# The first norm's scale and shift made as columns on TensorE, rows normalised and turned early

## The reference, cut to what matters

```python
cond = jax.nn.silu(c)                                   # 1 x 1024
mod = cond @ ada_w[layer] + ada_b[layer]                # ada_w: 1024 x 6144 for each layer
sh1, sc1, g1, sh2, sc2, g2 = jnp.split(mod, 6, axis=-1)
h = rms_norm(x, norm_mix[layer]) * (1 + sc1) + sh1      # the "first norm" of a layer
mix = mix_gla_gdn(h, ab_w_in[i], ...)                   # layer 0: begins with h @ ab_w_in
...
```

## Time and profile before

| what | value |
|---|---|
| median of 3 runs | 1464.72 us (1463.73 to 1470.1) |
| profiled execution, span | 1464.9 us |
| TensorE busy, share of the span | 87% |
| VectorE busy | 75% |
| ScalarE busy | 47% |
| first instruction of the first projection on TensorE | 62.41 us from the start |

### The profile page before, as it was taken

One profiled execution on the slowest core, in us unless ns is written; L12 is line 12 of the kernel. 1 busy time (PEld: TensorE's weight loads), 2 busy tenths in 40 slices (PEclk: granted clock), 3 DMA queues, 4 the chain that ended last, 5 costly groups with the idle time before them and its releaser, 6 DMA issues. The chain is left out here.

```text
span 1464.9 us, 15502 instructions
## 1 busy us (share of the span) xinstructions
PE 1280.1 (87%) x6000; PEld 970.2 (66%) x6000; DVE 1101.5 (75%) x1324; ACT 693.7 (47%) x890; POOL 311.9 (21%) x129
## 2 busy tenths in 40 slices
PE   4798997859899959999999967986898799999992
PEld 1476885659884557888888754444446588888882
DVE  2757986667783657999999946967357499999994
ACT  2222344222251316777777714227522377777770
POOL 2100000000000001555555310000000145555541
PEclk9799998979999959999999977997996799999997
DMA  9788626011703257999999546354006499999955
GB/s 328 259 266 272 214 96 211 19 44 58 259 2 130 87 219 273 375 391 382 373 378 373 225 157 240 115 203 183 1 29 258 142 358 385 377 381 392 380 206 191
DMA packets 63856, 338.17 MB, mean 231 GB/s; under 512 B 11837, under 2 KB 12350, under 8 KB 49700
## 3 DMA queue, kind: packets, MB, share of 16 engines
q1 hardware_dynamic: 51428, 311.00, 57.3%
q0 software_dynamic: 11536, 22.91, 4.5%
q10 hardware_dynamic: 816, 3.23, 0.6%
HBM read 325.64 MB, written 28.84 MB: 242 GB/s over the span
## 5 line engine op out<-in xcount | busy, mean ns | idle before, releaser
L1421 PE MATMUL ps<-ring_r,work_r 128*128 128x512 f32 x536 | 212.7, 397 | 0.0
L2455 DVE TENSOR_TENSOR ring_r<-ring,early_mod_r 128x2048 fp32r<-128x2048 f32 x76 | 188.7, 2512 | 21.2 <-ACT early_mod_r L1576 20.7
L1419 PE MATMUL ps<-early_mod_r,work_r 128*128 128x512 f32 x468 | 187.8, 401 | 7.7 <-DVE work_r L2758 4.7
L834 POOL TENSOR_TENSOR work<-work,early_mod 128x1024 f32<-128x1024 f32 x30 | 158.1, 5271 | 157.3 <-ACT work L1576 157.3
L1576 ACT ACTIVATE work<-ps 128x512 f32<-128x512 f32 (+3 forms) x121 | 80.5, 670 | 224.8 <-PE ps L1421 134.7
L1420 PE MATMUL ps<-early_mod_r,work_r 128*128 128x512 f32 x468 | 183.1, 391 | 0.0
L1576 ACT ACTIVATE work_r<-ring 128x2048 fp32r<-128x2048 f32 (+2 forms) x87 | 133.8, 1558 | 89.2 <-PE ps L946 89.2
L1576 ACT ACTIVATE early_mod_r<-ring 128x2048 fp32r<-128x2048 f32 x79 | 147.6, 1910 | 0.3 <-PE ps L1421 0.3
L937 PE MATMUL ps<-const,work 128*128 128x128 f32 x712 | 106.4, 293 | 44.2 <-DMA work<-h_rows,row_i 11.9
L1419 PE MATMUL ps<-work_r 128*128 128x512 f32 x324 | 132.9, 410 | 6.8 <-DVE work_r L2758 4.7
L937 PEld LDWEIGHTS ps<-const,work 128*128 128x128 f32 x712 | 90.1, 151 | 68.7 <-issue 15.0
(11 more groups left out here) (330 smaller groups left out, 2448.3 us busy)
## 6 DMA issues: line engine op xcount, KB each, us to landing
ring<-in_moe_w_up_dram SPq DMA_DIRECT2D x33, 2048.0 KB, 10.8
early_mod<-in_ada_w_dram SPq DMA_DIRECT2D x80, 512.0 KB, 4.4
ring<-in_moe_w_gate_dram SPq DMA_DIRECT2D x19, 2048.0 KB, 9.6
hT<-in_moe_w_down_dram SPq DMA_DIRECT2D x16, 2048.0 KB, 9.9
ring<-in_moe_w_down_dram SPq DMA_DIRECT2D x15, 2048.0 KB, 10.2
work<-in_moe_w_gate_dram SPq DMA_DIRECT2D x14, 2048.0 KB, 10.8
ring<-in_ab_w_in_dram SPq DMA_DIRECT2D x7, 2048.0 KB, 10.4
ring<-in_ada_w_dram SPq DMA_DIRECT2D x4, 2048.0 KB, 23.6
```

Of the source, the lines that this page charges most:

```text
L834: return nc.gpsimd.tensor_tensor(yb[buf], yb[buf], mod[:, 5 * D:6 * D], ALU.mult)
L1419: mm(out, a_lo, w_hi, start=first_, stop=False)
L1421: return mm(out, a_hi, w_lo, start=False, stop=last_)
L2455: v.tensor_tensor(half_of(l, m, half, True), half_of(l, m, half), highs[(2 * m + half) % MHIGHS].bitcast(F32), ALU.subtract).then_inc(SV.s ...
```

## The change

Shift and scale are no longer made as rows that are repeated on all partitions, but as columns: 16 columns of 128 values in one PSUM bank, features on the partitions. `ada_w[0][:, 0:2048]` arrives as eight row blocks k of 128 rows by 2048 columns (1 MB each, two in a ring slot). For each k, TensorE takes 16 blocks of 128 x 128 weights as the stationary operand and multiplies each by one column, `cond[:, k:k+1]`, adding into one column of the bank. The bias enters by one 16-column product before. The rows of x are multiplied by 1/rms as soon as it is known (DVE tiles 0 and 2, ACT tiles 1 and 3), turned by TensorE after k = 4 and k = 5, and kept turned in `xnT`. When the last k is done, DVE copies the shift column and forms the scale column, ACT writes the high part of each k block straight from `xnT` as scale * x + shift with the two columns as operands of each partition, and DVE makes the same in full and subtracts for the low part. POOL takes no part any more. The gain row, the bias row and the repeated silu(c) go; gain and bias come with the `c_cols` load (32 columns now). The first projection may start when k blocks 0 and 1 are ready. The thirteen small parameters are asked for when the first chunk of `ab_w_in` has landed, and the larger constants after the norm; their waits move to where they are used.

```diff
-            def first_mod():
-                pe.wait_ge(FIRST_DVE.sem, FIRST_DVE.at(0, "rep"))
-                for i, n in enumerate(FIRST):
-                    pe.wait_ge(chunk_in[i], 16)
-                    for k in range(4):
-                        mm(bank(i), cond_rep[:, k], slot(i)[:, 4 + k], start=(k == 0), stop=False)
...
+            def first_mod(lo, hi):
+                for k in range(lo, hi):
+                    pe.wait_ge(chunk_in[k // 2] if k % 2 else first_in[k // 2], 16)
+                    for n in range(2 * KD):
+                        ins = mm(bank(0)[:, n:n + 1], first_rows[k][:, cols(n)], cond[:, k:k + 1], start=False, stop=(k == KD - 1),
+                                 skip_group_check=True)
+                    ins.then_inc(FIRST_PE.sem, FIRST_PE.one(f"k{k}"))
...
-            first_mod()
-            pe.wait_ge(const_in, 16)
-            norm()
+            pe.wait_ge(ident_in, 16)
+            pe.wait_ge(cond_dve.sem, cond_dve.at(0, "silu"))
+            mm(bank(0)[:, 0:2 * KD], ident, first_bias, start=True, stop=False, skip_group_check=True)
+            first_mod(0, 5)
+            turn_first(0)
+            turn_first(1)
+            first_mod(5, 6)
+            turn_first(2)
+            turn_first(3)
+            first_mod(6, 8)
             project_ab()
...
-            load_columns(("ada", 0), a["ada_w"][0], [512 * n for n in FIRST])
+            for k in range(KD):
+                landed = chunk_in[k // 2] if k % 2 else first_in[k // 2]
+                sp.dma_start(first_rows[k], a["ada_w"][0].rearrange("(k p) f -> p k f", p=P)[:, k, 0:2 * D]).then_inc(landed, 16)
...
-                    sp.wait_ge(FIRST_PE.sem, FIRST_PE.at(0, f"m{c - RING}"))
+                    sp.wait_ge(FIRST_PE.sem, FIRST_PE.at(0, f"k{2 * (c - RING) + 1}"))
...
+                for k in range(KD):
+                    f(hT_high[:, k], xnT[:, k], ACT.Identity, bias=shift_col0[:, k:k + 1], scale=scale_col0[:, k:k + 1]
+                      ).then_inc(norm_act.sem, norm_act.one(f"hi{k}"))
+                    if k in (1, 3):
+                        high_part(k // 2)
...
+                dve.wait_ge(FIRST_PE.sem, FIRST_PE.at(0, "k7"))
+                v.tensor_copy(shift_col0, bank(0)[:, 0:KD]).then_inc(S.sem, S.one("shift"))
+                v.scalar_tensor_tensor(out=scale_col0, in0=bank(0)[:, KD:2 * KD], scalar=1.0, in1=first_gain,
+                                       op0=ALU.add, op1=ALU.mult).then_inc(S.sem, S.one("scale"))
...
+                for k in range(KD):
+                    v.tensor_scalar(hT_full[:, k], xnT[:, k], scale_col0[:, k:k + 1], shift_col0[:, k:k + 1], ALU.mult, ALU.add
+                                    ).then_inc(norm_dve.sem, norm_dve.one(f"full{k}"))
+                    dve.wait_ge(norm_dve.sem, norm_dve.at(0, f"full{k}"))
+                    dve.wait_ge(norm_act.sem, norm_act.at(0, f"hi{k}"))
+                    v.tensor_tensor(hT_low[:, k], hT_full[:, k], hT_high[:, k].bitcast(F32), ALU.subtract).then_inc(norm_dve.sem, norm_dve.one(f"lo{k}"))
+                    if k in (1, 3):
+                        low_part(k // 2)
...
-            nc.scalar.dma_start(const[:], a["consts"][:, NEARLY:NCONST]).then_inc(const_in, 16)
+            nc.scalar.dma_start(const[:, 0:2 * P], a["consts"][:, NEARLY:NEARLY + 2 * P]).then_inc(ident_in, 16)
...
-            nc.scalar.dma_start(early_mod[:, 0:NEARLY], a["consts"][:, 0:NEARLY]).then_inc(early_in, 16)
             first_norm()
             norm()
+            nc.scalar.dma_start(const[:, 2 * P:], a["consts"][:, NEARLY + 2 * P:NCONST]).then_inc(const_in, 16)
+            nc.scalar.dma_start(early_mod[:, 0:NEARLY], a["consts"][:, 0:NEARLY]).then_inc(early_in, 16)
```

More of the change, by code:

```diff
@@ L206, in build_block @@
         early_in = sem("early_in")
+        ident_in = sem("ident_in")
+        first_in = [sem(f"first_in{s}") for s in range(RING)]
         cond_in = sem("cond_in")
@@ L399, in build_block @@
         h = carve("work", TT, D)
[L401 to L404, removed]
+        xnT = work[:, 0:4096].rearrange("p (k n) -> p k n", k=KD)
+        gain2 = mod[:, 512:1536]
+        first_rows = [ring.rearrange("p s k f -> p (s k f)")[:, 2048 * k:2048 * k + 2048] for k in range(KD)]
         junk_wide = work[:, NWORK - D:NWORK]
@@ L894, in experts @@
                 pool.sem_inc(moe_done, 1)
[L896 to L904, removed]
+            nc.gpsimd.memset(side_pad, 0.0).then_inc(pad_ready, 1)
+            pool.wait_ge(chunk_in[0], 32)
             param(w2aug[0:SMALL + 1, :], a["gate_rows"])
@@ L982, in turn_rows_normed, with turn_first @@
                 ins.then_inc(RN_PE.sem, RN_PE.one("turned"))
[L984 to L998, removed]
+            def turn_first(t):
+                st = norm_act if t % 2 else norm_dve
+                pe.wait_ge(st.sem, st.at(0, f"xn{t}"))
+                if t >= 2:
+                    pe.wait_ge(norm_act.sem, norm_act.at(0, f"ev{t - 2}"))
+                    pe.wait_ge(norm_dve.sem, norm_dve.at(0, f"ev{t - 2}"))
+                for k in range(KD):
+                    ins = turn(bank(4 + 2 * (t % 2) + k // 4)[:, cols(k % 4)], x[:, t, cols(k)])
+                ins.then_inc(norm_pe.sem, norm_pe.one(f"turned{t}"))
             def project_ab():
-                pe.wait_ge(norm_act.sem, norm_act.at(0, "ev3"))
-                pe.wait_ge(norm_dve.sem, norm_dve.at(0, "ev3"))
                 def sums(ct):
@@ L1605, in first_norm @@
                 f(rstd[:], var[:], ACT.Abs_reciprocal_sqrt).then_inc(norm_act.sem, norm_act.one("root"))
+                act.wait_ge(norm_dve.sem, norm_dve.at(0, "rstd"))
+                for t in (1, 3):
+                    f(x[:, t], x[:, t], ACT.Copy, scale=rstd[:, t:t + 1]).then_inc(norm_act.sem, norm_act.one(f"xn{t}"))
+                for t in range(TT):
+                    act.wait_ge(norm_pe.sem, norm_pe.at(0, f"turned{t}"))
+                    f(xnT[:, 0:4, cols(t)], bank(4 + 2 * (t % 2), 4, P)).then_inc(norm_act.sem, norm_act.one(f"ev{t}"))
             def row_root(t):
```

121 lines of the change are left out of this document (39 added, 82 removed).

## The result

The changed kernel takes 1483.66 us (median of 4 runs, 1482.1 to 1486.57), the kernel before, run beside it, 1466.99 (4 runs, 1463.73 to 1470.1): ratio 1.0119, interval 1.0092 to 1.0145. It is slower by 16.7 us, 1.2%, and lies above the forecast range of 1467 to 1480. The three runs on which the forecast stood had their median 2.3 us lower, at 1464.72.

The account below looks back on a forecast made before the run. It took TensorE's own pace behind the first projection as the bound, so a later start is passed on: 69.6 + 4.3 = 73.9 instead of 62.41, 11.5 us later, span 1464.9 + 11.5 = 1476.4. Forecast time 1476 us, range 1467 to 1480.

Parts of the forecast that it names:

- The bound and the first block: First stage: the first projection's start is passed on almost whole; first row block there at 8.0 us, bounds 4.5 to 9.6.
- One-column products at 1.2 GHz: First stage on TensorE: 0.213 us per product at the lower clock, 6.8 us a row block, 54.6 us in all.
- Transposes 6.8, TensorE done at 69.6, tail 4.3: 32 transposes among the blocks take 6.8 us, TensorE ends at 69.6, then 4.3 us to the projection in place of 13.4.
- Queued work hidden, nothing absorbed, nothing starved: Behind the first stage: later weight chunks, side loads and constants are covered; TensorE's 7.5 us of waits swallow no delay.
- The sum: Whole kernel: first projection at 73.9 instead of 62.41, 11.5 us later, so span 1476.4; half-clock case, chance 0.58.
- Raised clock: First stage: both transpose stretches raise the clock for one block each, first projection at 67.1, about 1469.5 us; chance 0.21.
- Full clock: First stage: 2.4 GHz throughout, a block takes 3.4 us, first projection at 36.6, 25.8 us earlier, 1439 us; chance 0.07.
- Starved: Projection: late side loads and constants make DVE hold up a quarter's `low_part`, another 3 to 5 us, 1480; chance 0.10.
- absorbed: Behind the projection's start: TensorE's 7.5 us of waits shrink by most of theirs, 1468 us; chance 0.04.

Follow-up runs that it names:

- e3: Changed kernel with each first-stage product 128 columns wide instead of one, part of the scale and shift sums left out; 1463.62 us, ratio 0.9968 to the kernel before.
- e1: Kernel before with only NPAR raised from 1112 to 1160, work area 192 bytes further on; 1471.97 us, ratio 1.0036 to the kernel before.
- e2: Changed kernel with NPAR 1240 instead of 1160, work area 512 bytes from its old place; 1475.24 us, ratio 1.0058 to the kernel before.
- e9: Changed kernel with NPAR back at 1112, work area at its old place; 1479.28 us, ratio 1.0053 to the kernel before.
- e10: Changed kernel unchanged, measured again beside e9; 1481.86 us, ratio 1.0082 to the kernel before.
- e4: Changed kernel with first-stage products 16 columns wide instead of one, part of the sums missing; 1474.75 us, one execution.
- e5: e3 with all sums kept and NPAR 1240 instead of 1160; 1459.80 us, ratio 0.9937 to the kernel before.
- e6: e5 with SP's first three side loads issued ahead of the projection's second to fourth weight chunks; 1455.83 us, ratio 0.9918 to the kernel before.

## Why the prediction was wrong

**The bound and the first block: right.** The first row block was taken for 8.0 us; its products start at 7.86.

**One-column products at 1.2 GHz: right.** 0.213 us a MATMUL and 6.8 a block forecast; 34.29 us for five blocks and 6.83 for one measured. The Trainium skill, page "TensorE: Matmul & The Clock Gate", section "Why this matters for your kernels", holds that a TensorE kept busy without gaps gets the higher clock; 34 us of one-column or of sixteen-column products without a gap, at 0.214, speak against it for such narrow products, and the 128-column ones of e3, at 0.117, for it.

**Transposes 6.8, TensorE done at 69.6, tail 4.3: right.** Measured 7.3 us for the two timeline rows (each with its last MATMUL's own length), the last product's end at 69.24, 4.3 us to the projection: 73.54 instead of 73.9. The delay of the first projection is 11.1 us where 11.5 were forecast.

**Queued work hidden, nothing absorbed, nothing starved: right.** SP asked for the projection's chunks at the forecast times: the queue shows 21.70, 35.36 and, for the last, an issue that ends at 69.6.

```profile
21.70 0.39 SPq L686 DMA_DIRECT2D ring<-in_ab_w_in_dram  x1
35.36 0.37 SPq L697 DMA_DIRECT2D ring<-in_ab_w_in_dram  x1
35.77 33.87 SPq L686 DMA_DIRECT2D ring<-in_ab_w_in_dram  x3
```

**The sum: wrong.** The step that failed is "span 1464.9 + 11.5 = 1476.4": it takes the shift of the first projection for the only thing that changes. The forecast's first paragraph let 180 us "run at TensorE's own pace" and took for granted that this pace is the same in both kernels. It isn't: the change of NPAR from 1112 to 1160 moves the work area by 192 bytes, and that line had no term in the sum. e1 prices it at 4.7 us by medians (3 to 7 by the interval); e2 and e9 show the old pace restored. Of the miss of 1483.66 against 1476.0, 7.7 us, the place would then be 4.7, the three runs' low median 2.3, less 0.4 for the delay, with 1.1 unexplained. How much of it is the place in the changed kernel itself is measured less well: 3.8 us in the stretches without waits, 2.6 by the medians of e9 and e10. And e10 was only 12.2 us above the kernel before (8.7 to 15.4 by the interval), which the delay of 11.1 us alone would nearly give: scatter may be a part of the 7.7.

**The rivals.** *Raised clock*: the forecast gave it 0.21 and 67.1 us; e2 shows it at 67.11. What was wrong in it is "they may well go alike": in e9 the clock rises behind the first stretch and not behind the second. In both profiles of the changed kernel it rose behind neither. The same page of the Trainium skill, section "Part 4: PE-mode transpose", says that transposes don't raise the clock; e2, e4 and e9 show a block at the higher level right behind them, behind five of the ten stretches in the five profiles with narrow products. That the transposes are the cause is read from this order alone; no run took them out. *Full clock*: the one-column products ran at the lower level, and e3 shows what would have followed. The forecast's own sum for it was wrong: 36.6 us for the first projection leaves out that TensorE itself needs 8.0 + 27.3 + 3.4 for the products and transposes, with 0.2 and 4.3 behind them 43.2 us; e3 measured 46.42. And a gain at the start was taken for a gain at the end; in e3 and e5 the waits behind an early start grow. *Starved* and *absorbed*: waits of 7.9 and 7.5 us, equal within what they vary, speak against both.

**What stays open.** How the place lengthens a product: no run told apart which of the operands, the stationary or the moving one, pays for it. Of the operands only `work_r` moved, yet in the bare stretch the mean step behind L946, whose operands `ring_r` and `hT_r` stayed, went from 0.227 to 0.238 us, that behind L945 from 0.227 to 0.235, and that behind L944 only from 0.2325 to 0.2336 (lines of the kernel before). So it is more than the moved operand's own product. Which distance is the dearest depends on the stretch: 128 bytes cost less than 192 in the projection and more in the experts, and the whole times (ratios 1.0050 and 1.0036) don't separate them. And whether the transposes raise the clock in an execution is seen only afterwards.

## What to carry to other kernels

Read a diff's constants too: one that resizes a buffer moves all that lies behind it, and a stretch of products without waits, same count and same clock in both profiles, shows at once whether that costs something, while the difference of two medians of a few runs was here as uncertain as the price itself. Before moving TensorE work into many narrow products, look at which clock the profile grants such products; the same sums with 128 columns took about half the time here. And an earlier start is worth only what the engines behind it can follow: in e5 more than half of it was lost again by the projection's end, most of that in waits for loads queued too late, and e6 got nearly all of it back by reordering a queue.

## What the runs showed of the hardware that was not expected

- The place of the work area, moved in steps of 64 bytes, changes the pace of float32 split products: the bare stretch takes 78.12 us at distances of 0, 256 and 512 bytes and 78.88 to 79.42 at 64, 128 and 192, for the same MATMULs at the granted clock 1.00; nine stretches of the experts 405.8 to 407.6 and 409.3 to 411.2. The Trainium skill, page "SBUF — State Buffer", section "Operand start alignment", asks that an operand start at a multiple of its element size and says that its runs timed nothing; all places here obey it, since 64 bytes are a multiple of the 4 of a float32, and they differ by up to 1.7%.
- 160 MATMULs of 1 column (changed kernel) and 160 of 16 columns (e4) took the same 34.29 us, 0.214 a step, the lower level throughout; 160 of 128 columns (e3) took 19.93, and 32 of them behind that 3.74 us, where 32 of one column took 6.83.
- Behind the same sixteen transposes the clock was at the higher level for a block in some executions (e2, e4, first stretch of e9) and not in others (changed kernel, e10, second stretch of e9).
